# Three reordered stretches of a two-block transformer kernel: sparse attention's preparation, latent attention's norms and copies, and the memory part of the mix

## The reference

```
first block:
  hp = rmsnorm(x) @ w_in                      # u, q, kv, 24 head gates, 2 x 1024 mixing gates
  y_ssm = s5_mixer(u)                         # state space scan, gelu, GLU
  y_nsa = nsa_mixer(q, kv, gates)             # sparse attention
     kc = rmsnorm(gelu(blocks(k0) + pe @ w1) @ w2)   # 15 compressed keys per group, same for values
     out = g0 * attn(q, kc, vc) + g1 * attn(q, selected) + g2 * attn(q, window)
  x = x + (sigmoid(g)*(y_ssm @ w_proj_ssm) + sigmoid(g')*(y_nsa @ w_proj_nsa)) @ w_out
  x = x + relu(rmsnorm(x) @ w_up)^2 @ w_down
second block, layer 0 and 1:
  x = x + 0.5 * rmsnorm(swiglu(rmsnorm(x)))
  h = rmsnorm(x)
  tok = retention(h)  (layer 0)   or  latent attention(h)  (layer 1, 6 heads, 256 x 256, dense softmax)
  mem_out = attention of 4 heads of h over 256 memory rows
  x = x + rmsnorm(concat(tok, mem_out) @ w_o)      # tok is 768 wide, mem_out 256
  x = x + 0.5 * rmsnorm(swiglu(rmsnorm(x)))
```

## Time and profile before

| | us |
|---|---|
| runs, median of three | 1607.67 |
| profiled execution: whole time | 1609.99 |
| profiled execution: span of the core | 1608.20 |
| PE busy in the span | 1488.3 |
| DVE busy | 944.5 |
| ACT busy | 711.8 |
| POOL busy | 247.8 |

### The profile page before, as it was taken

One profiled execution on the slowest core, in us unless ns is written; L12 is line 12 of the kernel. 1 busy time (PEld: TensorE's weight loads), 2 busy tenths in 40 slices (PEclk: granted clock), 3 DMA queues, 4 the chain that ended last, 5 costly groups with the idle time before them and its releaser, 6 DMA issues.

```text
span 1608.2 us, 25066 instructions
## 1 busy us (share of the span) xinstructions
PE 1488.3 (93%) x9970; PEld 1347.2 (84%) x9970; DVE 944.5 (59%) x1370; ACT 711.8 (44%) x1155; POOL 247.8 (15%) x213
## 2 busy tenths in 40 slices
PE   3799967878999999999999899999999998899998
PEld 3688756777998889998889799988999887699986
DVE  7988325755664466654676566545565456565544
ACT  5323014534443354443644654445445354454443
POOL 6944200000120001110410111101111010021100
PEclk9799967788999999999999999999999999999999
DMA  6233133023555545555434355553555541235551
GB/s 241 105 106 131 66 129 105 1 69 118 181 185 190 196 162 184 183 196 186 145 131 144 105 188 188 205 191 135 185 191 203 190 182 53 71 140 183 199 190 69
DMA packets 36515, 242.04 MB, mean 151 GB/s; under 512 B 4176, under 2 KB 5328, under 8 KB 8784
## 3 DMA queue, kind: packets, MB, share of 16 engines
q1 hardware_dynamic: 34560, 235.55, 41.2%
q10 hardware_dynamic: 1872, 5.33, 1.0%
HBM read 239.58 MB, written 1.05 MB: 150 GB/s over the span
## 4 chain that ended last, share of the span: by engine, by line
PE 84%; DVE 7%; ACT 4%; POOL 3%; issue 1%; DMA 1%; ACTq 0%; DVEq 0%; POOLq 0%
PE ps L1779 48%; PE ps L1819 24%; PE ps L1992 2%; PE ps L1890 2%; DVE wlo L987 2%; PE ps L1966 2%; PE ps L1842 1%; PE ps L1843 1%; PE ps L1881 1%; POOL cosT L1683 1%; PE ps L1922 1%; PE ps L1982 1%; ACT whi L572 1%; POOL sinT L1685 1%; DVE alo L1331 1%
## 5 line engine op out<-in xcount | busy, mean ns | idle before, releaser
L987 DVE TENSOR_TENSOR wlo<-raw,whi 128x1024 fp32r<-128x1024 f32 (+1 forms) x434 | 519.0, 1238 | 330.6 <-ACT whi L572 330.5
L1779 PE MATMUL ps<-ahi,whi 128*128 128x256 f32 x2112 | 600.2, 284 | 34.4 <-DVE wlo L987 20.6
L572 ACT ACTIVATE whi<-raw 128x1024 fp32r<-128x1024 f32 (+1 forms) x434 | 426.8, 1032 | 445.6 <-PE ps L1779 243.4
L1779 PE MATMUL ps<-alo,whi 128*128 128x256 f32 x2112 | 595.3, 282 | 0.0
L1779 PE MATMUL ps<-ahi,wlo 128*128 128x256 f32 x2112 | 595.1, 282 | 0.0
L1779 PEld LDWEIGHTS ps<-ahi,whi 128*128 128x128 f32 x2112 | 401.7, 190 | 43.9 <-issue 19.7
L1779 PEld LDWEIGHTS ps<-alo,whi 128*128 128x128 f32 x2112 | 402.5, 191 | 0.7 <-issue 0.7
L1779 PEld LDWEIGHTS ps<-ahi,wlo 128*128 128x128 f32 x2112 | 401.4, 190 | 0.0
L1717 POOL TENSOR_TENSOR hlo<-fh,hhi 128x256 f32 (+3 forms) x104 | 85.8, 825 | 741.1 <-ACT hhi L806 543.3
L1390 DVE TENSOR_TENSOR fa<-ps,r 128x512 f32<-128x512 f32 x104 | 72.0, 692 | 173.8 <-PE ps L1779 173.6
L1819 PE MATMUL ps<-whi,hlo 128*128 128x512 f32 x480 | 150.8, 395 | 0.0
(11 more groups left out here) (338 smaller groups left out, 1547.8 us busy)
## 6 DMA issues: line engine op xcount, KB each, us to landing
raw<-in_w_gu SPq DMA_DIRECT2D x88, 1024.0 KB, 4.9
raw<-in_w_fd SPq DMA_DIRECT2D x44, 1024.0 KB, 4.9
raw<-in_w_up SPq DMA_DIRECT2D x16, 1024.0 KB, 4.9
raw<-in_w_dn SPq DMA_DIRECT2D x16, 1024.0 KB, 4.9
raw<-in_w_ret SPq DMA_DIRECT2D x13, 1024.0 KB, 5.0
raw<-in_w_mg SPq DMA_DIRECT2D x8, 1024.0 KB, 4.8
raw<-in_w_o SPq DMA_DIRECT2D x8, 1024.0 KB, 5.6
raw<-in_w_mem SPq DMA_DIRECT2D x4, 1024.0 KB, 4.9
```

Of the source, the lines that this page charges most:

```text
L572: nc.scalar.activation(whi[:, m % SPL, c], raw[:, n % RAW, c], ACT.Copy).then_inc(S("w_hi"), 1)
L987: ins = tt(wlo[:, m % SPL, c], raw[:, n % RAW, c], whi[:, m % SPL, c].bitcast(F32), ALU.subtract)
L1779: ins = mm(dst, lhsT, rhs, start=k == 0 and p == 0, stop=k == kt - 1 and p == len(pairs) - 1)
```

## The change

Nothing is computed differently, and no transfer is added. Instructions are moved, and one ACT table load is gone.

- Compression: on DVE the eight adds stand right behind the last memory unit's copy, ahead of `uT`, with a wait for all of POOL's products (`turned`, 32). On ACT the two moving DMAs stand ahead of the gelu and of the four other loads.
- Sparse preparation: DVE's preparation stands ahead of the four `w_ps` results; only the last two small instructions on `kcr` stay behind them. ACT's roots of `rq` and `sdk` stand ahead of the four splits and the root of `kcr` in their middle. PE's sum L1952 stands after the second `w_ps` unit.
- First mixer: `w_o` is taken in the order 3, 0, 1, 2. `mix_high(3)` and `mix_low(3)`, the memory part, stand before the first normalisation, with a wait for all six `ret_weight`, since `mhi` and `mlo` lie over the decay tables.
- Second mixer: the norm of ML[i] stands ahead of the maximum of ML[i+2], the copies likewise on ACT; PE's softmax steps are spread over more of the half units.

```diff
-O_ORDER = ((0, 1, 2, 3), (7, 4, 5, 6))
+O_ORDER = ((3, 0, 1, 2), (7, 4, 5, 6))
...
+            act.wait_ge(S("cx"), 1)
+            for g, src, dst in ((0, slice(0, 64), slice(64, P)), (1, slice(64, P), slice(0, 64))):
+                act.dma_start(CP[dst, :, g, 0:BLOCK_COLS], CX[src, :, 0:BLOCK_COLS]).then_inc(S("cp_moved"), 16)
+
             act.wait_ge(S("yv"), 4)
             act.wait_ge(S("c_done"), 16)
...
-            for c in range(4):
-                ahead(AT["w_ps", c])
-
             act.wait_ge(S("qk_sums"), 1)
             nc.scalar.activation(rq[:], PS[2][:, 0:16].rearrange("p (a b c) -> p a b c", a=TT, b=HG), ACT.Sqrt,
                                  bias=V["eps"], scale=1.0 / DH).then_inc(S("qk_root"), 1)
             nc.scalar.activation(sdk[:], two(3), ACT.Sqrt, bias=V["eps"], scale=1.0 / DH).then_inc(S("qk_root"), 1)
+            for c in range(4):
+                ahead(AT["w_ps", c])
+                if c == 1:
+                    act.wait_ge(S("kc_sums"), 1)
+                    nc.scalar.activation(kcr[:, 2, 0:N_CMP], PS[6][:, 96:96 + N_CMP], ACT.Sqrt, bias=V["eps"], scale=1.0 / DH)\
+                      .then_inc(S("kc_root"), 1)
...
                         act.wait_ge(S("att_out"), parts_out["mem0"])
+                        act.wait_ge(S("ret_weight"), RH)
...
                 unit_ahead(7)
+                mix_high(3)
                 normalise(0)
...
                 mix_high(2)
-                mix_high(3)
...
                 exps(ML[1])
                 copies(ML[0])
+                copies(ML[1])
                 exps(ML[2])
-                copies(ML[1])
                 exps(ML[3])
                 copies(ML[2])
-                mix_high(1, 0, VL[1])
                 exps(ML[4])
                 copies(ML[3])
+                mix_high(1, 0, VL[1])
...
             fill_result(FILL[N_STATE_TILES - 1])
+            dve.wait_ge(S("turned"), 2 * N_STATE_TILES)
+            dve.wait_ge(S("in_small"), 48)
+            for kv in range(2):
+                for g in range(NG):
+                    rows = slice(DH * g, DH * g + DH)
+                    for half in (1 - g, g):
+
+                        dst = CP[rows, kv, g] if half == g else CX[rows, kv]
+                        t0 = CMP_STRIDE * half
+                        ins = tt(dst[:, 0:BLOCK_COLS].rearrange("p (c j) -> p c j", j=CMP_STRIDE),
+                                 KC[rows, kv, t0:t0 + BLOCK_COLS].rearrange("p (c j) -> p c j", j=CMP_STRIDE),
+                                 over(pe_kv[rows, kv, t0:t0 + CMP_STRIDE], N_CMP), ALU.add)
+            ins.then_inc(S("cx"), 1)
...
-            for c in range(4):
-                bank = group(AT["w_ps", c])
-                dve.wait_ge(S("mix_gate"), 8)
-                tt(mrg[:, 2 * c:2 * c + 2], bank, mg[:, 2 * c:2 * c + 2], ALU.mult).then_inc(S("evac"), 1)
-
+            dve.wait_ge(S("kvc_done"), 1)
+            dve.wait_ge(S("nsa_zeroed"), 1)
+            cp(kcr[:, 0, 0:N_CMP], PS[6][:, 64:64 + N_CMP]).then_inc(S("kc"), 1)
+            for i in range(4):
+                ins = cp(VC[32 * i:32 * i + N_CMP, i, :], PS[7][32 * i:32 * i + N_CMP, 64:64 + P])
+            chain(ins)
             dve.wait_ge(S("qk_root"), 2)
...
+            for c in range(4):
+                bank = group(AT["w_ps", c])
+                dve.wait_ge(S("mix_gate"), 8)
+                tt(mrg[:, 2 * c:2 * c + 2], bank, mg[:, 2 * c:2 * c + 2], ALU.mult).then_inc(S("evac"), 1)
+
             dve.wait_ge(S("kc_root"), 1)
...
-                    dve.wait_ge(S("mix_hi"), u + 1)
+                    dve.wait_ge(S("mix_hi"), (u + 1) % 4 + 1)
+                    if u == 3:
+                        dve.wait_ge(S("ret_weight"), RH)
...
                 values_in(1)
+                mix_low(3)
                 statistics(0)
...
                 norm(ML[0])
+                norm(ML[1])
                 prep(ML[2])
-                norm(ML[1])
-                result(VL[0])
                 prep(ML[3])
                 norm(ML[2])
+                result(VL[0])
+                prep(ML[4])
+                norm(ML[3])
                 result(VL[1])
                 mix_low(1, 0)
-                prep(ML[4])
-                norm(ML[3])
-                result(VL[2])
                 prep(ML[5])
                 norm(ML[4])
                 ahead(AT["w_o", 7])
                 norm(ML[5])
+                result(VL[2])
                 result(VL[3])
...
+                if c == 1:
+                    pe.wait_ge(S("kc_sq"), 1)
+                    mm(PS[6][:, 96:96 + N_CMP], C["bones"], kcr[:, 1, 0:N_CMP], start=True, stop=True).then_inc(S("kc_sums"), 1)
...
+                def first_pair():
                     pe.wait_ge(S("att_out"), parts_out["mem1"])
-                    transposes(ML[0])
-                    scores(ML[2])
-                    for i in range(1, 4):
+                    for i in range(2):
                         transposes(ML[i])
-                        values(VL[i - 1])
-                        scores(ML[i + 2])
-
-                def rest(i):
-                    if i < 6:
-                        transposes(ML[i])
-                    values(VL[i - 1])
+                        scores(ML[2 + i])
+
+                def second_pair():
+                    values(VL[0])
+                    transposes(ML[2])
+                    scores(ML[4])
+                    values(VL[1])
+                    transposes(ML[3])
+                    scores(ML[5])
+                    need(1)
+
+                def third_pair():
+                    transposes(ML[4])
+                    values(VL[2])
+                    values(VL[3])
+
+                def fifth():
+                    transposes(ML[5])
+                    values(VL[4])
...
+                     between={(0, 1): first_pair, (1, 0): second_pair, (1, 1): third_pair, (2, 0): fifth,
+                              (2, 1): lambda: values(VL[5])},
                      turn=3)
...
-                    down(3, AT["w_o", 0], 4, mhi, mlo, lambda u: pe.wait_ge(S("mix_lo"), u + 1), between={(1, 0): last_pair})
+                    down(3, AT["w_o", 3], 4, mhi, mlo, lambda u: pe.wait_ge(S("mix_lo"), u + 1), between={(1, 0): last_pair},
+                         turn=3)
```

More of the change, by code:

```diff
@@ L101 @@
 NOT_GROUP = ("w_dn", "w_fd", "w_out", "w_o", "w_c1")
-LAST_DOWN = [AT["w_out", 3], AT["w_dn", 15], AT["w_fd", 10], AT["w_o", 3], AT["w_fd", 21], AT["w_fd", 32],
+LAST_DOWN = [AT["w_out", 3], AT["w_dn", 15], AT["w_fd", 10], AT["w_o", 2], AT["w_fd", 21], AT["w_fd", 32],
              AT["w_o", 6], AT["w_fd", 43]]
@@ L661, in _ @@
                 act.dma_start(dst[:], A[name]).then_inc(S("in_nsa"), 16)
-            act.wait_ge(S("cx"), 1)
-            for g, src, dst in ((0, slice(0, 64), slice(64, P)), (1, slice(64, P), slice(0, 64))):
-                act.dma_start(CP[dst, :, g, 0:BLOCK_COLS], CX[src, :, 0:BLOCK_COLS]).then_inc(S("cp_moved"), 16)
             act.wait_ge(*done(AT["w_c1", 1]))
@@ L683, in _ @@
             nc.scalar.activation(sdk[:], two(3), ACT.Sqrt, bias=V["eps"], scale=1.0 / DH).then_inc(S("qk_root"), 1)
+            for c in range(4):
[4 more added lines that the diff above has]
+                      .then_inc(S("kc_root"), 1)
             act.wait_ge(S("gate_logit"), 1)
             nc.scalar.activation(gate[:], gate[:], ACT.Sigmoid).then_inc(S("gate"), 1)
-            act.wait_ge(S("kc_sums"), 1)
-            nc.scalar.activation(kcr[:, 2, 0:N_CMP], PS[6][:, 96:96 + N_CMP], ACT.Sqrt, bias=V["eps"], scale=1.0 / DH)\
-              .then_inc(S("kc_root"), 1)
             def exps(s):
@@ L1134, in _ @@
             fill_result(FILL[N_STATE_TILES - 1])
-            for k in range(4):
-                dve.wait_ge(S("c_done"), 8 * (k // 2 + 1))
-                stt(uT[:, k], uT[:, k], V["d_skip"][:, k:k + 1], two(4 + k // 2)[:, k % 2], ALU.mult, ALU.add)\
-                    .then_inc(S("yv"), 1)
-            dve.wait_ge(S("yg"), 2)
-            tt(yglo[:], yg[:], yghi[:].bitcast(F32), ALU.subtract).then_inc(S("yglo"), 1)
+            dve.wait_ge(S("turned"), 2 * N_STATE_TILES)
             dve.wait_ge(S("in_small"), 48)
@@ L1153, in _ @@
             ins.then_inc(S("cx"), 1)
+            for k in range(4):
+                dve.wait_ge(S("c_done"), 8 * (k // 2 + 1))
+                stt(uT[:, k], uT[:, k], V["d_skip"][:, k:k + 1], two(4 + k // 2)[:, k % 2], ALU.mult, ALU.add)\
+                    .then_inc(S("yv"), 1)
+            dve.wait_ge(S("yg"), 2)
+            tt(yglo[:], yg[:], yghi[:].bitcast(F32), ALU.subtract).then_inc(S("yglo"), 1)
             dve.wait_ge(S("vv_tr"), 1)
@@ L1185, in _ @@
             ins.then_inc(S("gate_logit"), 1)
-            dve.wait_ge(S("kvc_done"), 1)
-            dve.wait_ge(S("nsa_zeroed"), 1)
-            cp(kcr[:, 0, 0:N_CMP], PS[6][:, 64:64 + N_CMP]).then_inc(S("kc"), 1)
-            for i in range(4):
-                ins = cp(VC[32 * i:32 * i + N_CMP, i, :], PS[7][32 * i:32 * i + N_CMP, 64:64 + P])
```

(11 more changed lines are left out.)

7 lines of the change are left out of this document (1 added, 6 removed).

## The result

Four runs of the changed kernel took 1580.98, 1585.50, 1587.59 and 1589.10 us, median 1586.55; four of the kernel before had the median 1607.87. The ratio is 0.9869 with a 95% interval of 0.983 to 0.9908: 21.3 us less, between 15 and 27. Forecast were 1592.5 us (15.2 less) and a range of 1584 to 1600, which holds it. The profiled execution took 1580.98 us (span 1579.1, granted clock 0.965).

The account below looks back on a forecast made before the run. PE bounds the kernel (84% of the last chain), so time is won where it waits or runs slowly. 4.8 + 7.0 - 0.6 + 4.0 = 15.2 us less gives 1592.5 us against the median 1607.67; range 1584 to 1600 (8 in 10).

Parts of the forecast that it names:

- Compression, 4.8: Before the compression matmuls: adds and moving DMAs issued earlier let PE start 4.8 us sooner, bounds 4.0 and 8.2.
- the landing: Compression: time from first issue of the moving DMAs to PE's start, taken as 4.0 us instead of 4.7.
- The wait of 1.5 to 3 us that was to show there: Sign in the new profile: PE's wait before the compression matmuls is 1.5 to 3 us instead of 10.7.
- Preparation, 7.0 with a 1.3 us stall: Sparse attention: scores start 7.0 us earlier, including a 1.3 us PE stall at the third `w_ps` unit; bounds 5.6 to 8.3.
- the 1 to 2 that were to show: Sign in the new profile: a PE wait of 1 to 2 us stands before the third `w_ps` unit.
- First mixer, -0.6: First mixer: one `mlo` ahead of the first statistics costs 0.6 us; the order of `w_o` removes nothing; bounds 0 or 2.6.
- Second mixer, 4.0: Second mixer: norms ahead of maxima gain 2.9 us from waits, 5.3 without the low-clock stretch; 4.0 taken, bounds 1.8 and 5.4.
- The 2.4 us set for the low stretch: Second mixer: 4 us at granted 0.57 behind the longest wait cost 2.4 us of the same work.
- the clock gives more: Rival, 15%: first scores and compression start at 2.4 GHz, 7 to 8 us more gained, 1585 us.
- Turn-taking: Compression: DVE's adds and POOL's squares alternate by whole instructions; the rival without it gains 2.7 us more, 1589.8 us, 10%.
- Stalls that eat it: Rival, 12%: preparation stalls the third and fourth unit, second mixer wins its lower bound; 7.2 us gained, 1600.5 us.
- Slower: Rival, 3%: the `w_ps` stall and small gaps keep PE at 1.2 GHz through the projection after sparse attention; 1617.5 us.

Follow-up runs that it names:

- x_comp: The kernel before with the compression part of the change alone (eight adds and two moving DMAs first): 1601.58 us, ratio 0.9961.
- x_prep: The kernel before with the sparse preparation alone (DVE's preparation ahead of the four results, key sum behind the second unit): 1599.90 us, ratio 0.9962.
- y_sq: The changed kernel with POOL's squares of q and k waiting until the eight adds are done: 1586.22 us, ratio 0.9878.

## Why the prediction was right, step by step

The sum was 6 us below the measured difference of the medians. Most of its steps were right, and here is each with its size.

- *Compression, 4.8*: measured 5.8, since it is 9.24 or 9.25 us from `mv` in x_comp and in every profile of the changed kernel, against 15.05 before (14.9 to 15.5 in the other profiles with the old order). The chain was the forecast one to 0.1 us on DVE (second add 2.9, adds 5.5 us in all). The mis-sized term is the landing, taken at 4.0 us with 3.2 as its lower bound, and measured at 3.1. PE is done with its small transposes 0.3 us before the landing, so a still quicker one would have given at most 0.3 us more. The wait of 1.5 to 3 us that was to show there was 0.3, because most of PE's idle time (5.1 us) now stands one step earlier, ahead of the transposes.
- *Preparation, 7.0 with a 1.3 us stall*: x_prep gave 7.0 and 1.36. In the whole change it is 7.2 to 7.5 us with a stall of 0.2 to 0.3, not the 1 to 2 that were to show: the two units ahead of it were slower, so there was less to wait for. That this term came out all the same is partly luck, since the slower units and the shorter stall nearly cancel.
- *First mixer, -0.6*: -0.6 (1.23 instead of 0.64 at the first heads, 4.1 at the last, nothing from the order of `w_o`).
- *Second mixer, 4.0*: the waits were forecast as 0.9, 1.1 and 2.5 and measured as 0.89, 1.12 and 2.04. Like against like the part gives 2.9 us, so the 2.9 "from waits" was the number to take; the 1.1 added for the clock was a mean over two states, and both come in either kernel. The 2.4 us set for the low stretch is also not what rows 10 give: 4.00 us at 0.57 are 1.7 us lost. Between the states it measured 2.7 with either mixer.
- *The clock*: this is where the rest came from. Steady sum: `mv` to the first FFN 201.85 us before (three profiles) and 185.0 after (four), 16.9; mixers -0.6 and +2.9; together **19.2 us** against the 15.2 forecast. The 4.0 between them are 1.0 of landing, 2.3 from there to `w_ps` (2.6 by the gates' clock and 0.3 ahead of them, less the 0.7 that PE now waits for `yslo`), 1.8 at the scores and in the attention, and -1.1 in the second mixer. PE's busy time shows the clock's part directly: from `mv` to the first FFN it is 154.6 us before and 151.0 after for the same 864 matmuls, 3.6 us of 16.7 in these two profiles, and idle time gave the other 13.1. This is about half of the rival "the clock gives more". It was right for the first scores (1.13 instead of 2.05 us) and wrong for the compression, which stayed at 1.2 GHz, as did most of `w_ps`'s first half; it did not name the gate matmuls, where the largest piece came from. The sum had put this term at nothing up to the scores.
- *Turn-taking*: the rival without it fell with y_sq. *Stalls that eat it* fell: every new wait that was forecast was at or below its size; the 0.7 us for `yslo` is one that nobody forecast. *Slower* fell.

The 19.2 us lie within each of the three intervals (14.8 to 27.3, 15 to 26 and 15 to 23 us). The 21.3 us between the medians also hold what the states of those few runs add, so the nearer number is 19.2. The other 9.9 us between the two profiled spans are, to 0.2 us, 1.75 of start-up, 4.5 of the FFN, 3.4 of the second mixer's low stretches and 0.3 in the first mixer, differences that repeated profiles of one kernel show as well.

## What to carry to other kernels

Before you explain a difference between two traces, profile the same kernel again: here a third of it lay in states that either kernel can be in. The reordering was worth what the wait chain said, to about 1 us in each part, plus a clock term that no wait shows (3.6 of 16.7 us up to the first FFN); a clock term of this kind also made a true gain of 2.55 us (POOL's squares moved) disappear. So read the granted clock of the thin matmuls behind each edit, and judge small edits where PE is thinly used by the next stage's start, not by the wait that they remove.
